# Four parts of the last v product among the first score blocks of a hybrid layer

## The chip, the core and the metric

The kernel runs on one core of a Trainium2 chip. The metric is the time of one execution on the device in microseconds (us). The core has five engines with instruction streams of their own: PE (TensorE, matrix products and transposes), DVE (VectorE), ACT (ScalarE), POOL (GpSimd) and SP (SyncE, which here only issues DMAs). They meet through semaphores alone.

## What is computed

One step of an encoder layer on 1024 prompt tokens and 32 sample tokens, model width 1024: a SwiGLU block, a mixer with three groups of heads, a second SwiGLU block and a norm. The mixer's second group, "fox", is attention with eight heads of 64 and a forget gate. Cut to that group:

```
h = rms(x); proj = h @ w_in                       # q, k, v, f_logit among its columns
q = head_rms(q, gq);  k = head_rms(k, gk)
F = cumsum(log_sigmoid(f_logit + b_f))            # past rows ahead of it
s = q @ k^T * 64**-0.5 + F_q - F_k                # causal
y = softmax(s) @ v
outputs also: k, v and log f of every token
```

## The kernel before

All 1056 tokens (1024 and 32) are handled together, with features on the partitions. The mixer runs over eight steps: two for the convolution, four "fox" pairs of two heads each (`g` = 0 to 3, called the first to the fourth pair here), and two memory pairs. A pair has two halves.

**Projections.** For each pair nine products are made, q, k and v, each in three chunks of 384, 384 and 288 tokens: n = 0 to 8. A product is 24 matmuls: eight blocks of the model width (`KT` = 8), and for each block three matmuls that multiply split numbers (high by high, low by high, high by low; lines 252 to 254). The last of them, n = 8, is the third chunk of v, 128x288, and goes to bank 2. After n = 7 PE transposes four tiles of k (`turn_tokens(0)`), after n = 8 the other five (`turn_tokens(1)`, `(2)`).

**Maxima by query.** `scores(n)`, n = 0 to 17, gives the scores of one tile of queries of one head; `smax(n)` on DVE adds -F and takes the row maximum (line 1692, tile scores_minusF, in an order of its own: the units 0 and 1 are the sample tokens, 2 to 9 the first head's eight tiles, with 128 to 1024 keys). Two areas of PSUM serve them in turn: `scores(n)` waits for `smax(n-2)`. `scores(0)` waits for the rounded k (`khi`, ACT line 1130, tile k_hi_twice) and `scores(1)` for ACT's copies of all k tiles by token (line 1147, tile k_by_token), whose banks it overwrites. `turn_tokens(3)` to `(5)` transpose v, eight tiles and the last of 32 tokens; `(4)` and `(5)` wait for the third chunk of v to be copied out (`vcopied`, ACT line 1196, tile vT). `turn_max` (lines 2074, 2075) turns maxima into rows, and ACT copies these.

**Weighted sum.** When the first head's maxima are all turned and copied, `keyed(0)` starts (line 2102). From there PE makes scores by key, ACT their exponentials, and PE the sums with v (line 2118); the second head's `scores(10)` to `(17)` stand among them. The next pair's nine products follow on PE.

The order on every engine is written out by hand; nothing is scheduled. On DVE the roundings of k (`k_twice`, `k_lo`, lines 1664 and 1671) stand right ahead of `smax(0)`. On ACT the stream in the loop over n is: copy v's chunk, round k after n = 7 (`k_hi`), copy tile groups (`tokens`). POOL rounds the next pair's weights when the ninth product and `k_lo` are done (lines 799 to 803). In the first pair only, PE also transposes the forget gates by token (line 2150); only after the first of these may SP load minusF (-F of a head, on every partition), which `smax(0)` waits for: it issues it at line 636.

Of the kernel before, what the change touches and what calls it, by code (L numbers as in the profile page):

```python
# [31 lines left out]
def hybrid_step(nc, i, o):  # L32
# [12 lines left out]
    KT = D // P  # L45
# [17 lines left out]
    with ctx:  # L63
# [78 lines left out]
        hh = sb("h_hi", [P, KT, T], F32R, ms_)  # L142
        hl = sb("h_lo", [P, KT, T], F32R, ms_)
# [112 lines left out]
        block = ctx.enter_context(nc.Block())  # L256
# [9 lines left out]
        def span(kind, n):  # L266

            what, _, c = PROJ[kind][n]
            return (0, NMEM) if kind == "mem" and what != "q" else CHUNKS[c]
# [583 lines left out]
        def _(act):  # L853
# [256 lines left out]
            def attend(g):  # L1110
                kind, it = ATTEND[g]
# [29 lines left out]
                def tokens(q):  # L1141
                    what, t0, nt, b = TT[kind][q]
                    act.wait_ge(A["tturned"], tt0 + q + 1)
                    n = tile_rows(kind, t0)
                    src = bank(b, nt * P, n).rearrange("p (t n) -> p t n", t=nt)
                    if what == "k":
                        act.activation(ktok[0:n, t0:t0 + nt, :], src, ACT.Copy).then_inc(A["tcopied"], 1)
                        return
                    for j in range(PAIR):
                        mm = act.activation(VO[0:n, t0:t0 + nt, j, half_rows(j)], src[:, :, half_rows(j)], ACT.Copy)  # L1150
                    mm.then_inc(A["tcopied"], 1)
# [40 lines left out]
                for n, (what, _, c) in enumerate(PROJ[kind]):  # L1192
                    s, w = span(kind, n)
                    act.wait_ge(A["proj"], proj0 + n + 1)
                    if what == "v":
                        act.activation(vT[:, s:s + w], bank(PBANK[kind][n], w), ACT.Copy).then_inc(A["vcopied"], 1)
                    else:
                        m = NORMED[kind].index(n)
                        if m >= 2:
                            act.wait_ge(A["sums"], sq0 + m - 1)  # L1200
                        act.activation(hsq[:, m % 2, 0:w], bank(PBANK[kind][n], w), ACT.Square)\
                            .then_inc(A["squares"], 1)
                    for m in SUMS_AFTER[kind].get(n, []):
                        head_rough(m)
                    if g == 0 and n == 1:
                        forget_log()
                    if n == (4 if kind == "fox" else 3):
                        past_keys()
                    if kind == "mem" and it == 0 and n == 1:
                        for h in range(2):  # L1210
                            act.wait_ge(mp["dve"], 5 + h)
                            act.activation(memh[:, 4 * h:4 * h + 4, :], memf[h], ACT.Copy).then_inc(mp["hi"], 1)
                    if n in (2, 3, 4):
                        q_hi(n - 2)
                    if kind == "fox" and n == 7:
                        k_hi()
                        act.wait_ge(A["stored"], upto(NSTORED, g))
                        tokens(0)
                    if kind == "fox" and n == 8:
                        tokens(1)  # L1220
                        tokens(2)
                if kind == "mem":
                    k_hi()
                    act.wait_ge(A["stored"], upto(NSTORED, g))
                    tokens(0)
                    tokens(1)
                else:
                    tokens(3)
                    tokens(4)
                    tokens(5)  # L1230
                for x in range(3):
# [552 lines left out]
        def _(pe):  # L1784
# [25 lines left out]
                pe.wait_ge(NORM[n]["sums"], sums_before(n, c) + 3)  # L1810
                pe.matmul(bank(MBANK + c, w), onesD[:, :], nsum[:, 0:w], start=True, stop=True).then_inc(NORM[n]["mean"], 1)

            def product(b, block, x_hi, x_lo, s, w, fresh=None):


                for k in range(KT):
                    if fresh:
                        n, c = fresh
                        pe.wait_ge(NORM[n]["lo"], KT * c + k + 1)
                    ks = slice(k * P, (k + 1) * P)  # L1820
                    mm = split3(pe, bank(b, w), whi[:, block, ks], wlo[:, block, ks], x_hi[:, k, s:s + w],
                                x_lo[:, k, s:s + w], k == 0, k == KT - 1)
                return mm
# [159 lines left out]
            def attend(g):  # L1983
# [137 lines left out]
                for n, (what, b, c) in enumerate(PROJ[kind]):  # L2121
                    s, w = span(kind, n)
                    pe.wait_ge(W["lo"], 3 * v + b + 1)
                    bank_free(n)
                    xh, xl = x.get((kind, what), (hh, hl))
                    if (kind, it) == ("mem", 0) and n == 3:
                        pe.wait_ge(mp["lo"], 2)
                    if (kind, it) == ("mem", 0) and n in (2, 3):
                        pe.wait_ge(mp["dve"], 6)
                    product(PBANK[kind][n], b, xh, xl, s, w).then_inc(A["proj"], 1)  # L2130
                    for m in SUMS_AFTER[kind].get(n, []):
                        head_sums(m)
                    if n == (4 if kind == "fox" else 3):
                        turn_past()
                    if (kind, it) == ("mem", 0) and n == 1:
                        pe.wait_ge(A["mixed"], 18 * g)
                        turn_memory()
                    if kind == "fox" and n == 7:
                        turn_tokens(0)
                if kind == "fox":  # L2140
                    turn_tokens(1)
                    turn_tokens(2)
                    if g == 0:
                        pe.wait_ge(fg["dve"], 10)
                        pe.wait_ge(A["tcopied"], 1)
                        for n, (src, at) in enumerate(((FL, 320), (FN, 400))):
                            for t in range(NT + n):
                                c0, w = (t * P, P) if t < PT else ((SEQ + PAST, DEC), (SEQ, PAST))[t - PT]
                                b = 512 * 3 + at + t * FH
                                mm = pe.transpose(PS[0:w, b:b + FH], src[:, c0:c0 + w], ident[0:FH, 0:FH])  # L2150
                            mm.then_inc(fg["turned"], 1)
                else:
                    turn_tokens(0)
                    turn_tokens(1)
                scores(0)
                scores(1)
                if kind == "fox":
                    turn_tokens(3)
                scores(2)
                scores(3)  # L2160
                if kind == "fox":
                    turn_tokens(4)
                scores(4)
                if kind == "fox":
                    turn_tokens(5)
                pe.wait_ge(A["vcopied"], upto(NV, g + 1))
                turn_max(0, 2, 0)
                turn_max(1, 2, DEC).then_inc(A["mturned"], 1)
# [84 lines left out]
```

## Time and profile before

| | |
|---|---|
| median of 3 runs | 2306.92 us (2306.61 to 2307.15) |
| the profiled execution | 2311.69 us |
| its span, first to last instruction | 2309.6 us |
| PE busy | 92% |
| DVE busy | 49% |
| ACT busy | 34% |
| mean granted TensorE clock | 0.946 |

The rows further below come from that one profiled execution. Its own time is 4.77 us above the median, and 2.1 us of it lie outside the span. A timeline row gives start, duration, engine, line, operation, output and inputs, shapes and count; in square brackets is the idle time ahead of it on its engine, and what ended it. The ends of matmuls are modelled and overlap; starts are the better measure of how they follow each other.

### The profile page before, as it was taken

How to read it: one execution, taken by the hardware profiler on the slowest of the kernel's cores; microseconds unless marked ns; L12 is line 12 of the kernel's file. 1: busy time of each engine (PE TensorE's matmuls, PEld its weight loads, DVE VectorE, ACT ScalarE, POOL GpSimd, SP SyncE). 2: the span in 40 equal slices, each digit the busy share in tenths (PEclk: the TensorE clock that was granted, in tenths of full speed). 3: DMA queues.
4: the chain of work that ended last, by engine and by line, in shares of the span. 5: the costliest groups of instructions: out<-in, count | busy, mean ns of one | idle time of the engine just before them, and what ended most of it. 6: DMA issues, size and time to landing. Idle time of an engine off the chain costs nothing.

```text
span 2309.6 us, 36830 instructions
## 1 busy us (share of the span) xinstructions
PE 2117.2 (92%) x15188; PEld 1995.8 (86%) x15188; DVE 1134.0 (49%) x1989; ACT 781.1 (34%) x1315; POOL 346.0 (15%) x175
## 2 busy tenths in 40 slices
PE   4599999999999888899999789966999999999996
PEld 4599999999999888776876567965999999999996
DVE  6855566556320162544544555177655665643103
ACT  5332222324221230454455453043232232433213
POOL 0000000004444522101101202000000000144440
PEclk7799999999999989899999779977999999999997
DMA  4512222228532326321220125032222222385222
GB/s 149 140 57 83 84 79 89 70 76 310 166 122 92 112 36 40 88 61 41 57 61 22 46 90 177 9 104 84 77 72 84 84 74 90 115 296 168 87 70 85
DMA packets 214774, 222.16 MB, mean 96 GB/s; under 512 B 27913, under 2 KB 156553, under 8 KB 214097
## 3 DMA queue, kind: packets, MB, share of 16 engines
q1 hardware_dynamic: 214608, 219.81, 31.5%
q8 instruction: 122, 2.00, 0.4%
q14 instruction: 44, 0.35, 0.0%
HBM read 169.98 MB, written 49.80 MB: 95 GB/s over the span
## 4 chain that ended last, share of the span: by engine, by line
PE 85%; DVE 7%; DMA 3%; ACT 2%; issue 1%; SPq 1%; POOL 0%; DVEq 0%; ACTq 0%
PE banks L252 24%; PE banks L253 24%; PE banks L254 24%; PE banks L2118 4%; PE banks L2060 1%; PE banks L2102 1%; PE banks L1831 1%; DMA x_again<-x_spill 1%; PE banks L2103 1%; DVE scores_minusF L1692 1%; DMA out_conv_state_sample<-conv_in 1%; PE banks L1997 1%; DVE hforms_lo L1459 1%; DVE hforms_f L1443 1%; PE banks L2218 0%
## 5 line engine op out<-in xcount | busy, mean ns | idle before, releaser
L252 PE MATMUL banks<-hforms_hi,w_hi 128*128 128x264 f32 x2112 | 604.8, 286 | 65.6 <-DVE hforms_lo L1459 44.6
L253 PE MATMUL banks<-hforms_lo,w_hi 128*128 128x264 f32 x2112 | 605.8, 287 | 0.0
L254 PE MATMUL banks<-hforms_hi,w_lo 128*128 128x264 f32 x2112 | 604.1, 286 | 0.0
L252 PEld LDWEIGHTS banks<-hforms_hi,w_hi 128*128 128x128 f32 x2112 | 402.5, 191 | 68.8 <-issue 35.7
L779 POOL TENSOR_TENSOR w_lo<-w_raw,w_hi 128x1024 fp32r<-128x1024 f32 x88 | 218.6, 2486 | 1386.6 <-ACT w_hi L984 1386.6
L254 PEld LDWEIGHTS banks<-hforms_hi,w_lo 128*128 128x128 f32 x2112 | 401.9, 190 | 0.0
L253 PEld LDWEIGHTS banks<-hforms_lo,w_hi 128*128 128x128 f32 x2112 | 401.5, 190 | 0.0
L254 PE MATMUL banks<-acts_a,w_lo 128*128 128x264 f32 x896 | 256.3, 286 | 0.0
L252 PE MATMUL banks<-acts_a,w_hi 128*128 128x264 f32 x896 | 254.2, 284 | 1.9 <-DVE acts_a L1477 1.9
L253 PE MATMUL banks<-acts_a,w_hi 128*128 128x264 f32 x896 | 255.0, 285 | 0.0
L252 PE MATMUL banks<-h_hi,w_hi 128*128 128x384 f32 (+1 forms) x576 | 198.8, 345 | 21.7 <-DVE h_lo L1311 10.0
L984 ACT ACTIVATE w_hi<-w_raw 128x1024 fp32r<-128x1024 f32 x88 | 93.2, 1059 | 349.8 <-PE banks L254 308.1
L253 PE MATMUL banks<-h_lo,w_hi 128*128 128x384 f32 (+1 forms) x576 | 189.6, 329 | 0.0
L254 PE MATMUL banks<-h_hi,w_lo 128*128 128x384 f32 (+1 forms) x576 | 188.7, 328 | 0.0
L252 PEld LDWEIGHTS banks<-acts_a,w_hi 128*128 128x128 f32 x896 | 170.0, 190 | 2.4 <-issue 2.4
L1493 DVE SCALAR_TENSOR_TENSOR xT<-banks,xT 128x264 f32<-128x264 f32 x64 | 23.9, 432 | 298.0 <-PE banks L254 298.0
L254 PEld LDWEIGHTS banks<-acts_a,w_lo 128*128 128x128 f32 x896 | 168.3, 188 | 0.0
L253 PEld LDWEIGHTS banks<-acts_a,w_hi 128*128 128x128 f32 x896 | 168.2, 188 | 0.0
L254 PE MATMUL banks<-acts_b,w_lo 128*128 128x264 f32 x512 | 146.5, 286 | 0.0
L253 PE MATMUL banks<-acts_b,w_hi 128*128 128x264 f32 x512 | 145.7, 285 | 0.0
L252 PE MATMUL banks<-acts_b,w_hi 128*128 128x264 f32 x512 | 145.1, 283 | 0.0
L252 PEld LDWEIGHTS banks<-h_hi,w_hi 128*128 128x128 f32 x576 | 111.5, 194 | 30.3 <-issue 20.8
(257 smaller groups left out, 3963.6 us busy)
## 6 DMA issues: line engine op xcount, KB each, us to landing
w_raw<-in_w_ffn_down SPq DMA_DIRECT2D x88, 512.0 KB, 4.2
w_raw<-in_w_ffn_gate SPq DMA_DIRECT2D x48, 512.0 KB, 5.2
w_raw<-in_w_ffn_up SPq DMA_DIRECT2D x48, 512.0 KB, 5.2
act_rows<-act_f SPq DMA_DIRECT2D x44, 528.0 KB, 2.8
acts_f<-act_rows SPq DMA_DIRECT2D x44, 528.0 KB, 5.0
xT<-x_spill SPq DMA_DIRECT2D x3, 4224.0 KB, 16.4
w_raw<-in_w_in SPq DMA_DIRECT2D x20, 512.0 KB, 5.9
x_spill<-xT SPq DMA_DIRECT2D x4, 2112.0 KB, 9.3
```

The lines of the kernel that those rows point to most:

```text
L252: eng.matmul(out, w_hi, x_hi, start=first, stop=False, skip_group_check=added)
L253: eng.matmul(out, w_hi, x_lo, start=False, stop=False, skip_group_check=added)
L254: return eng.matmul(out, w_lo, x_hi, start=False, stop=last, skip_group_check=added)
L779: pool.tensor_tensor(wlo[:, e % 4, :], raw[:, e % 4, :], whi[:, e % 4, :].bitcast(F32), ALU.subtract)\
L984: act.activation(whi[:, e % 4, :], raw[:, e % 4, :], ACT.Copy).then_inc(f["wd_hi"], 1)
L1443: dve.scalar_tensor_tensor(q[:, first:last + 1:last - first, :], x.rearrange("p (h n) -> p h n", h=2), gain[:, 2 * n, k:k + 1], nr[:, s:s ...
L1459: dve.tensor_tensor(HL[z][:, :, kk, :], FT[:, m % 2, 0:7, :], HH[z][:, :, kk, :].bitcast(F32), ALU.subtract).then_inc(f["forms_lo"], 1)
L1493: dve.scalar_tensor_tensor(xT[:, d, s:s + QC], bank(DBANK[e], QC), 0.5, xT[:, d, s:s + QC], ALU.mult, ALU.add).then_inc(f["resid"], 1)
L1692: dve.tensor_tensor_reduce(junk[0:rows, 0:w], PS[0:rows, b:b + w], nF[0:rows, j, k0:k0 + w], 1.0, -3e38, ALU.add, ALU.max, m).then_inc(A[" ...
L1831: mm = pe.matmul(bank(4 + c, QC), onesD[:, :], q[:, k, :], start=k == 0, stop=k == KT - 1)
L1997: pe.matmul(bank(6 + m % 2, w), onesH[:, :], hsq[:, m % 2, 0:w], start=True, stop=True)\
L2118: pe.matmul(PS[:, 512 * ob + oc:512 * ob + oc + w], VO[0:kr, vo, j, :], PRT[0:kr, (b0 + n) % 4, 0:w], start=first, stop=last, skip_group_c ...
```

## The change

The ninth product of a fox pair is no longer made whole behind the eighth. The loop over n ends at n = 8, `product` takes the blocks that it shall do, and `last_v` makes two of the eight blocks (six matmuls) at a time: one part ahead of `scores(0)`, one behind `turn_tokens(3)`, one behind `scores(2)`, one behind `scores(3)`. The product's semaphore follows the fourth part. `turn_tokens(1)` and `(2)` now stand ahead of all parts, and so do, in the first pair, the transposes of the forget gates. `turn_tokens(4)` and `(5)` stand together behind `scores(4)`. ACT copies k's tiles and the first four of v ahead of v's third chunk. The memory pairs keep their order. Lines below the edit have other numbers: PE's line 2035 is 2032 afterwards, 2060 is 2057, 2063 is 2060, 2150 is 2154.

```diff
@@ ACT, attend(g) @@
                     if kind == "fox" and n == 7:
                         k_hi()
                         act.wait_ge(A["stored"], upto(NSTORED, g))
-                        tokens(0)
-                    if kind == "fox" and n == 8:
-                        tokens(1)
-                        tokens(2)
+                        for q in range(4):
+                            tokens(q)
...
                 else:
-                    tokens(3)
                     tokens(4)
                     tokens(5)
@@ PE @@
-            def product(b, block, x_hi, x_lo, s, w, fresh=None):
+            def product(b, block, x_hi, x_lo, s, w, fresh=None, steps=range(KT)):
...
-                for k in range(KT):
+                for k in steps:
...
+                    if kind == "fox" and n == 8:
+                        break
                     product(PBANK[kind][n], b, xh, xl, s, w).then_inc(A["proj"], 1)
...
+                def last_v(steps):
+
+                    s, w = span(kind, 8)
+                    return product(PBANK[kind][8], 2, hh, hl, s, w, None, steps)
...
                             mm.then_inc(fg["turned"], 1)
+                    last_v(range(0, 2))
+                    scores(0)
+                    scores(1)
+                    turn_tokens(3)
+                    last_v(range(2, 4))
+                    scores(2)
+                    last_v(range(4, 6))
+                    scores(3)
+                    last_v(range(6, KT)).then_inc(A["proj"], 1)
+                    scores(4)
+                    turn_tokens(4)
+                    turn_tokens(5)
                 else:
                     turn_tokens(0)
                     turn_tokens(1)
-                scores(0)
-                scores(1)
-                if kind == "fox":
-                    turn_tokens(3)
-                scores(2)
-                scores(3)
-                if kind == "fox":
-                    turn_tokens(4)
-                scores(4)
-                if kind == "fox":
-                    turn_tokens(5)
+                    for n in range(5):
+                        scores(n)
```

PE in the third pair before, from the ninth product's last matmul to `scores(4)` (the rows with k_hi_twice and mask_bf are the score blocks, those with ident and vT the transposes of v; an "x4" means four in a row):

```order
L254 MATMUL banks<-h_hi,w_lo 128x288
L2035 MATMUL banks<-ident,kT 128x128 x4
L2035 MATMUL banks<-ident,kT 32x128
L2060 MATMUL banks<-k_hi_twice,q_hi_lo 32x160
L2063 MATMUL banks<-mask_bf,ident_bf 32x32
L2060 MATMUL banks<-k_hi_twice,q_hi_lo 32x160
L2063 MATMUL banks<-mask_bf,ident_bf 32x32
L2035 MATMUL banks<-ident,vT 128x128 x4
L2060 MATMUL banks<-k_hi_twice,q_hi_lo 128x128
L2063 MATMUL banks<-mask_bf,ident_bf 128x128
L2060 MATMUL banks<-k_hi_twice,q_hi_lo 128x256
L2063 MATMUL banks<-mask_bf,ident_bf 128x128
```

The same engine and pair now, from `turn_tokens(3)` to the score block of 128x128 (`scores(2)`):

```order
L2032 MATMUL banks<-ident,vT 128x128 x4
L252 MATMUL banks<-h_hi,w_hi 128x288
L253 MATMUL banks<-h_lo,w_hi 128x288
L254 MATMUL banks<-h_hi,w_lo 128x288
L252 MATMUL banks<-h_hi,w_hi 128x288
L253 MATMUL banks<-h_lo,w_hi 128x288
L254 MATMUL banks<-h_hi,w_lo 128x288
L2057 MATMUL banks<-k_hi_twice,q_hi_lo 128x128
L2060 MATMUL banks<-mask_bf,ident_bf 128x128
```

Six matmuls of the product stand ahead of `scores(2)`, where none stood; six more stand ahead of `scores(3)`, and six ahead of `scores(4)`.

ACT in the third pair before, from the rounding of k to the copies of v by token:

```order
L1130 ACTIVATE k_hi_twice<-kT 64x1184 x2
L1147 ACTIVATE k_by_token<-banks 128x512
L1196 ACTIVATE vT<-banks 128x288
L1147 ACTIVATE k_by_token<-banks 128x512
L1147 ACTIVATE k_by_token<-banks 32x128
L1150 ACTIVATE v_and_ones<-banks 128x4x64 x4
L1150 ACTIVATE v_and_ones<-banks 32x64 x2
```

And now:

```order
L1130 ACTIVATE k_hi_twice<-kT 64x1184 x2
L1147 ACTIVATE k_by_token<-banks 128x512 x2
L1147 ACTIVATE k_by_token<-banks 32x128
L1150 ACTIVATE v_and_ones<-banks 128x4x64 x2
L1196 ACTIVATE vT<-banks 128x288
L1150 ACTIVATE v_and_ones<-banks 128x4x64 x2
L1150 ACTIVATE v_and_ones<-banks 32x64 x2
```

The copy of v's third chunk (vT, 128x288) has moved behind all copies of k and the first two of v.

PE in the first pair before, behind the ninth product, with the forget gates (logf_rows, minusF_rows):

```order
L254 MATMUL banks<-h_hi,w_lo 128x288
L2035 MATMUL banks<-ident,kT 128x128 x4
L2035 MATMUL banks<-ident,kT 32x128
L2150 MATMUL banks<-ident,logf_rows 128x8 x8
L2150 MATMUL banks<-ident,logf_rows 32x8
```

And now, behind the eighth product:

```order
L254 MATMUL banks<-h_hi,w_lo 128x384
L2032 MATMUL banks<-ident,kT 128x128 x8
L2032 MATMUL banks<-ident,kT 32x128
L2154 MATMUL banks<-ident,logf_rows 128x8 x8
L2154 MATMUL banks<-ident,logf_rows 32x8
```

The forget gates' transposes are ahead of the whole ninth product now.

## Rows read from the trace of the kernel before

**Rows 1.** The page: the chain that ended last, by engine.
```profile
PE 85%; DVE 7%; DMA 3%; ACT 2%; issue 1%; SPq 1%; POOL 0%; DVEq 0%; ACTq 0%
```

**Rows 2.** Timeline of the third pair, all engines, up to the first maximum.
```profile
1133.79 0.60 PE L2035 MATMUL banks<-ident,kT 128*128 128x128 f32 x4
...
1134.37 2.40 ACT L1130 ACTIVATE k_hi_twice<-kT 64x1184 fp32r<-64x1184 f32 x2
1135.59 2.81 DVE L1671 TENSOR_TENSOR k_lo_and_one<-kT,k_hi_twice 64x1184 fp32r<-64x1184 f32 x2 [0.98 <-ACT k_hi_twice L1130]
1136.79 0.60 ACT L1147 ACTIVATE k_by_token<-banks 128x512 f32<-128x512 f32 x1
...
1137.40 0.71 PE L2035 MATMUL banks<-ident,kT 128*128 128x128 f32 x5
1137.60 0.41 ACT L1196 ACTIVATE vT<-banks 128x288 f32<-128x288 f32 x1 [0.21 <-PE banks L254]
...
1137.87 0.32 PE L2060 MATMUL banks<-k_hi_twice,q_hi_lo 128*32 128x160 f32 x1
1138.04 0.74 ACT L1147 ACTIVATE k_by_token<-banks 128x512 f32<-128x512 f32 x2
...
1138.43 0.31 DVE L1692 CUSTOM_DVE_ANT_0 scores_minusF<-banks,minusF 32x160 f32<-32x160 f32 x1
```

**Rows 3.** The chain that ended last, in order of time, in the ninth product.
```profile
1137.17 0.13 PE banks L252
...
1137.43 0.13 PE banks L254
```

**Rows 4.** Timeline of the third pair, from `scores(1)` to the maximum of unit 5.
```profile
1138.83 0.26 PE L2060 MATMUL banks<-k_hi_twice,q_hi_lo 128*32 128x160 f32 x1 [0.54 <-ACT k_by_token L1147]
...
1139.97 0.29 DVE L1692 CUSTOM_DVE_ANT_0 scores_minusF<-banks,minusF 128x128 f32<-128x128 f32 x1 [0.40 <-PE banks L2063]
...
1140.38 0.42 PE L2060 MATMUL banks<-k_hi_twice,q_hi_lo 128*128 128x384 f32 x1
...
1141.11 0.49 PE L2060 MATMUL banks<-k_hi_twice,q_hi_lo 128*128 128x512 f32 x1
...
1141.71 0.69 DVE L1692 CUSTOM_DVE_ANT_0 scores_minusF<-banks,minusF 128x512 f32<-128x512 f32 x1 [0.15 <-PE banks L2063]
```

**Rows 5.** Timeline of the third pair, from the last maximum of the first head.
```profile
1145.88 1.22 DVE L1692 CUSTOM_DVE_ANT_0 scores_minusF<-banks,minusF 128x1024 f32<-128x1024 f32 x1
...
1147.17 0.32 PE L2074 MATMUL banks<-ident,row_max 128*65 128x128 f32 x1 [1.05 <-DVE row_max L1692]
...
1148.17 0.50 PE L2102 MATMUL banks<-q_hi_lo,k_hi_twice 128*128 128x512 f32 x1 [0.68 <-ACT q_hi_and_max L1164]
```

**Rows 6.** PE by stretches: length, busy (instructions), granted clock, DMA share, GB/s.
```profile
1138.00:1139.00 1.00, 0.46 (x4) 1.00 0.00 0
1145.80:1148.10 2.30, 0.64 (x2) 1.00 0.00 0
1149.00:1153.00 4.00, 4.00 (x14) 0.57 0.00 0
961.00:972.00 11.00, 8.19 (x31) 0.53 1.10 294
```

**Rows 7.** Timeline of the first pair: ACT, SP's queue, DVE and PE.
```profile
955.41 0.60 ACT L1147 ACTIVATE k_by_token<-banks 128x512 f32<-128x512 f32 x1
...
956.65 0.68 PE L2150 MATMUL banks<-ident,logf_rows 8*128 8x8 f32 x9
...
957.41 0.81 SPq L636 DMA_DIRECT2D minusF<-negF_rows  x2
...
963.42 0.31 DVE L1692 CUSTOM_DVE_ANT_0 scores_minusF<-banks,minusF 32x160 f32<-32x160 f32 x1 [4.90 <-DMA minusF<-negF_rows]
...
963.79 0.47 PE L2060 MATMUL banks<-k_hi_twice,q_hi_lo 128*128 128x128 f32 x1 [4.67 <-DVE row_max L1692]
...
967.68 0.69 DVE L1692 CUSTOM_DVE_ANT_0 scores_minusF<-banks,minusF 128x512 f32<-128x512 f32 x1 [0.80 <-PE banks L2063]
```

## The prediction

> **What bounds the kernel now.** I read the page's chain first: PE carries 85% of it and DVE 7% [rows 1], so what is not PE's own rate is mostly waits for DVE. A pair's timeline shows where DVE is the bound: between the end of the nine products and `keyed(0)`. In the third pair the ninth product's last matmul starts at 1137.43 and is done at 1137.56 [rows 3], and `keyed(0)` starts at 1148.17 [rows 5]; in 10.6 us PE has only score blocks and transposes to make. The first, second and fourth pairs have the same stretch, in the second and fourth with the same waits to 0.02 us.
>
> The reader should see who holds that stretch. ACT's rounding of k ends at 1134.37 + 2.40 = 1136.77, DVE's `k_lo` ends at 1135.59 + 2.81 = 1138.40, and the first maximum starts at 1138.43, 0.03 us later [rows 2]. So at its start the chain of maxima is bound by DVE's `k_lo`, not by the ninth product, which ran beside it: **the product is hidden today**. The end is 1145.88 + 1.22, then a transpose at 1147.17 and ACT's copy [rows 5]. In between DVE is nearly gapless: it waits 0.50 us for the second unit (`scores(1)` could start only at 1138.83, after ACT's copies of k [rows 4]), 0.40 us for the third and 0.15 us for the sixth [rows 4]. That is 1.05 us in all, which is all that a perfect feed by PE could save in a pair.
>
> **What the change does in the second to fourth pair.** The step is 24 matmuls, spaced 0.13 us (1137.17 to 1137.43 is two of them [rows 3]): 3.1 us of PE. None is removed. I go along PE with the third pair's times.
>
> *Ahead of `scores(0)`.* The four transposes at 1133.79 are over by 1134.37; the five others take 0.45 us more (1137.40 to 1137.87 [rows 2]), so the first part runs from 1134.85 to 1135.65. Then `scores(0)` waits for the rounded k until 1136.8. PE idles 1.2 us where it had the product. The first maximum stays at 1138.43, since `k_lo` is untouched: gain nothing, loss nothing.
>
> *`scores(1)`.* It waits for three copies of k tiles. ACT had v's chunk (0.41 us) and a wait for it between them; now they go 1136.79 + 0.60 + 0.74 = 1138.13 [rows 2]. So `scores(1)` starts at 1138.19, 0.64 us earlier than 1138.83 [rows 4], and DVE's first gap of 0.50 us closes. Between `scores(0)` and this PE idles another 1.0 us.
>
> *`scores(1)` to `scores(5)`.* Before: 1141.11 - 1138.83 = 2.28 us [rows 4]. Added: 18 matmuls by 0.131 = 2.36 us, some 0.1 us for three switches (an estimate: 0.03 us a switch, from the starts around the product), and the copy of v's third chunk. That copy now follows the product's end directly and `turn_tokens(4)` waits for it: 0.41 us and some 0.2 us of latency [rows 2], less the 0.33 us of `scores(4)` between them, so 0.3 us. That is 5.04 us, and `scores(5)` starts at 1138.19 + 5.04 = 1143.23, 2.12 us later than 1141.11. The sixth maximum moves from 1141.71 to 1143.83 with it.
>
> *Behind it.* From the sixth maximum on DVE goes without gaps (five of them, 5.4 us to 1147.10), each unit's scores being ready two ahead. Nothing is given back, so `keyed(0)` is **2.1 us later** in each of three pairs: 6.4 us. ACT's v copies and the stores through SP's queue move too, but `keyed(0)` has them done by 1146. POOL starts the next pair's weights some 3.5 us later, and they take 10.3 us; the next products come some 35 us after that, which covers it. Queued behind PE's waits in this piece are only score blocks, and DVE waits for those alone.
>
> Bounds for one pair: 2.36 - 0.64 = 1.7 us, if switches and the copy cost nothing, and 2.5 us, if the copy's wait is twice as long. I take 2.1.
>
> **The first pair** is bound by a DMA. The first maximum waits 4.90 us for minusF, whose load SP issues at 957.41, when the first transposes of the forget gates are done [rows 7]. These now need only ACT's first copy (955.41 + 0.60 = 956.01) and no longer stand behind five transposes, so they start at 956.05 instead of 956.65: 0.6 us earlier, and minusF and the first maximum too (962.8). The first two parts lie in waits. The other two come behind the DMA's end, at a time when PE's clock has fallen: from 961 to 972 it was granted 0.53 of full speed [rows 6], that is, 1.2 GHz after 4.67 us without work [rows 7]. Now PE would be idle for some 3.1 us there. At half clock 12 matmuls are 12 by 0.26 = 3.1 us, with the copy's wait 3.4 us, less 0.6: +2.8 us at the sixth maximum. At full clock the whole would be faster than now, since from the first to the sixth maximum the third pair takes 3.28 us and this one 4.26 [rows 2, 4, 7]: 3.28 + 1.6 + 0.3 less the 0.9 us of the early transposes and of ACT's copies is 4.3, so -0.6, and 0.7 us more from larger units at full clock: -1.3. The row it is nearest to is the fallen clock, and part of the late maxima may then already run at 2.4 GHz: I take **+2.3 us**, with -1.3 and +2.8 as ends.
>
> **The clock in the new gaps.** Today PE idles 1.05 and 0.68 us ahead of `keyed(0)` [rows 5] and is busy 0.64 of 2.30 us there; the clock then falls to 1.2 GHz, and over 4.00 us it is 0.57 [rows 6]: 4.0 by 0.43 = 1.7 us of full work lost. All four pairs show it. The short gap at 1138 (busy 0.46 of 1.00 us) drew no fall [rows 6]. The new gaps, 1.2 and 1.0 us around `scores(0)`, are as deep as the first kind. A fall right behind them meets the stretch where PE is the bound, so it costs the same 1.7 us. It depends on how the gaps lie; I expect it in two of three pairs, and that one of the present falls behind the maxima fails to come, as places shift: **net one, +1.7 us**, between -1.7 and +5.1.
>
> The Trainium skill (TensorE: Matmul & The Clock Gate, "What's actually happening") says that the activity monitor runs free and does not start anew with the kernel, so that the number of slow matmuls differs between runs. By that rule this term is a draw of each run rather than a fixed cost; the runs of before, within 0.54 us of each other, do not show such a spread.
>
> **The sum.** 6.4 + 2.3 + 1.7 = +10.4 us. Against the profiled execution that is a span of 2309.6 + 10.4 = 2320.0; the difference goes over to the median, 2306.92 + 10.4 = **2317.3 us**.
>
> **The rivals.**
> *A, no new fall of the clock.* The new gaps leave the clock up and the first pair's shorter idle too: 6.4 - 1.3 = +5.1, 2312.0 us. For it: a shorter gap at 1138 drew none. Against it: gaps of this depth did, four times.
> *B, not slower.* The parts keep PE busier just ahead of `keyed(0)`, and the falls of the clock behind the maxima no longer come. Each is worth 1.7 us [rows 6], so from A all four give 5.1 - 6.8 = -1.7, 2305.2 us; it decides from the third one on. For it: those falls are a matter of how little PE does. Against it: the 2.1 us that are idle or nearly so behind the last score block are the same, and the parts end 4 us earlier.
> *C, two falls in a row.* The half clock lasts over all of `scores(1)` to `scores(5)`, 3.9 us of work in three pairs: 6.4 + 2.8 + 11.7 = +20.9, 2327.8 us. For it: in the first pair PE was busy at half clock for eight of the eleven us and did not recover [rows 6]. Against it: 1149 to 1153 is one short fall.
> The Trainium skill (Perfetto Trace Analysis, "Matmul Optimizations") says that the engine scales with its use and that matmuls should run back to back in batches, which speaks against cutting this product; by that rule the outcome would be C's.
> *D, the parts fill gaps after all.* DVE's 1.05 us of gaps are closed and the parts cost PE nothing. That would need the score blocks two units ahead of DVE at units 2 to 4; with 0.29 to 0.56 us a unit on DVE and 0.8 us a part on PE they cannot be. It would give 2306.92 - 3.2 = 2303.7 us.
>
> **How the numbers follow.** Main case 0.62 (2313 to 2321), A 0.17, B 0.08, C 0.08, D 0.02, rest 0.03. A measurement of this kernel can tell 0.2%, 4.6 us, from no change: slower means over 2311.5. The main case, C and most of A are slower: 0.80. Within 0.2%: the low side of A and most of B, 0.15. Faster: D and some of B, 0.05. The range runs from 2309 to 2322; it leaves out C, D and most of B.
>
> **What the profile of after would show.** For the steps: a third pair in which the first maximum still follows `k_lo` by 0.03 us, the second one without a gap, gaps of DVE of about 1.0, 0.6 and 0.7 us ahead of the third to fifth and some 0.9 ahead of the sixth, `turn_tokens(4)` waiting for vT, and 2.1 us more from `k_lo` to `keyed(0)`; SP's minusF 0.6 us earlier in the first pair; a clock of 0.5 somewhere between `scores(1)` and `scores(5)`. It would be wrong if the first maximum itself moved (ACT's or DVE's part would then not be what holds it), or if the maxima behind the sixth had gaps that took up the delay.

## The result, and the profile after

The changed kernel takes 2320.66 us (median of 5 runs, 2314.54 to 2323.07) against 2307.15 us before (5 runs, 2306.61 to 2309.01). The ratio is 1.005, 95% interval 1.0037 to 1.0063: slower by half a percent. The profiled execution is at 2323.07 us, the slowest of the five; its span is 2321.0 us against 2309.6. These five runs lie 8.5 us apart, the five of before 2.4. That alone does not make the spread a mark of the change: in three later sets of runs the kernel before was itself 6.6, 12.2 and 5.5 us apart (35, 29 and 15 runs).

The page of after; busy times of PE, DVE and ACT are as before to 2 us, so no engine does more. The second row is the chain by engine, to be held against [rows 1]:

```profile
span 2321.0 us, 36830 instructions
...
PE 86%; DVE 6%; ACT 3%; DMA 2%; issue 2%; POOL 0%; SPq 0%; DVEq 0%; ACTq 0%
```

Time is best read from two distances that every fox pair has: from the start of `k_lo` on DVE to the start of `keyed(0)` on PE (the stretch that the change touches), and from there to the next pair's `k_lo` (the weighted sum and eight products, which it does not touch). Worked out from the timelines, in us:

| pair | k_lo to keyed(0), before | after | keyed(0) to next k_lo, before | after |
|---|---|---|---|---|
| first | 20.68 | 22.39 | 73.32 | 74.30 |
| second | 12.59 | 16.29 | 74.80 | 73.30 |
| third | 12.58 | 14.72 | 73.38 | 73.33 |
| fourth | 12.59 | 16.25 | | |

The first two columns differ by 1.71 + 3.70 + 2.14 + 3.66 = 11.21 us, the last two by -0.57. Ahead of the first `k_lo` after is 1.46 us late (955.66 against 954.20), behind the fourth `keyed(0)` 0.72 us short. Together that is the span's 11.38 us. So the loss is where the change is.

The third pair of after, which answers to [rows 2] and [rows 4], with DVE, PE and ACT; `k_lo` is line 1668 here and the maxima 1689, score blocks are line 2057:

```profile
1141.94 2.80 DVE L1668 TENSOR_TENSOR k_lo_and_one<-kT,k_hi_twice 64x1184 fp32r<-64x1184 f32 x2 [0.98 <-ACT k_hi_twice L1130]
...
1143.37 0.23 PE L2057 MATMUL banks<-k_hi_twice,q_hi_lo 128*32 128x160 f32 x1 [1.30 <-DVE k_lo_and_one L1668]
...
1144.42 0.26 PE L2057 MATMUL banks<-k_hi_twice,q_hi_lo 128*32 128x160 f32 x1 [0.70 <-ACT k_by_token L1147]
...
1144.77 0.31 DVE L1689 CUSTOM_DVE_ANT_0 scores_minusF<-banks,minusF 32x160 f32<-32x160 f32 x1
...
1146.35 0.29 DVE L1689 CUSTOM_DVE_ANT_0 scores_minusF<-banks,minusF 128x128 f32<-128x128 f32 x1 [0.79 <-PE banks L2060]
...
1147.38 0.42 DVE L1689 CUSTOM_DVE_ANT_0 scores_minusF<-banks,minusF 128x256 f32<-128x256 f32 x1 [0.74 <-PE banks L2060]
...
1148.23 0.41 ACT L1196 ACTIVATE vT<-banks 128x288 f32<-128x288 f32 x1 [2.15 <-PE banks L254]
...
1148.48 0.56 DVE L1689 CUSTOM_DVE_ANT_0 scores_minusF<-banks,minusF 128x384 f32<-128x384 f32 x1 [0.66 <-PE banks L2060]
1148.69 0.77 PE L2032 MATMUL banks<-ident,vT 128*128 128x128 f32 x5 [0.25 <-ACT vT L1196]
...
1150.19 0.69 DVE L1689 CUSTOM_DVE_ANT_0 scores_minusF<-banks,minusF 128x512 f32<-128x512 f32 x1 [1.15 <-PE banks L2060]
```

PE stands still for 1.30 us where the product was, and for 0.70 us behind `scores(0)`. (The profile names `k_lo` as what released `scores(0)`; by the times it is ACT's rounding of k, which ends at the same moment.) DVE starts its maxima 2.83 us after `k_lo`'s start, as before, and then waits for PE four times: 0.79, 0.74, 0.66 and 1.15 us, where it waited 0.40, 0, 0 and 0.15.

In the second and fourth pair the clock fell in addition. (A "fall" here is a stretch in which the granted clock of PE is at 1.2 instead of 2.4 GHz, that is, 0.5 in the profile.) PE by stretches (length, busy, granted clock, DMA share, GB/s), four us from about `scores(1)` on in the second, third and fourth pair:

```profile
1055.00:1059.00 4.00, 4.00 (x21) 0.57 0.46 135
1145.00:1149.00 4.00, 3.75 (x31) 1.00 0.50 139
1232.50:1236.50 4.00, 4.00 (x20) 0.57 0.46 135
```

At 0.57 PE gets through 21 and 20 instructions, at full clock through 31. These two pairs take 16.29 and 16.25 us and the third 14.72: a fall costs 1.55 us there.

### The profile page after: what moved, and what is told of

Read it like the earlier page. It is cut to its first block, busy times and chain, and to the rows that moved or that the text cites. A ratio compares the mean times of both kernels' runs of the same rounds, so it can differ in the third digit from the quotient of the medians.

```text
span 2321.0 us, 36830 instructions
## 1 busy us (share of the span) xinstructions
PE 2119.2 (91%) x15188; PEld 1997.7 (86%) x15188; DVE 1134.0 (49%) x1989; ACT 780.5 (34%) x1315; POOL 345.8 (15%) x175
## 4 chain that ended last, share of the span: by engine, by line
PE 86%; DVE 6%; ACT 3%; DMA 2%; issue 2%; POOL 0%; SPq 0%; DVEq 0%; ACTq 0%
PE banks L252 25%; PE banks L253 25%; PE banks L254 25%; PE banks L2115 4%; PE banks L1828 1%; PE banks L2099 1%; PE banks L2057 1%; DVE scores_minusF L1689 1%; DMA x_again<-x_spill 1%; PE banks L2100 1%; DMA out_conv_state_sample<-conv_in 1%; PE banks L1994 1%; DVE hforms_lo L1456 1%; DVE hforms_f L1440 1%; PE banks L1793 0%
```

## The experiments

The medians of the kernel before were not the same in all sets of runs (2308.47, 2311.69 and 2311.14 us in the three below; 2307.15 above), so each run is judged by its ratio to the runs of before of its own set, and by the two distances in its profile. Several expectations gave absolute times from the 2307 us of before and miss for that reason alone; where a miss means more, it is said.

**The theory.** The ninth product is free where it was, since DVE's `k_lo` ends later than it; behind the first score block it is paid in full, since DVE then works on units shorter than a part. The clock's fall in the new gap comes on top. **Rivals**: ACT's new order is what delays; the cut as such or the wait for v's copy, not the amount of late matmuls; the clock alone.

**The whole product ahead of `scores(0)`.** The rest of the change stays.

```diff
-                    last_v(range(0, 2))
+                    last_v(range(0, KT)).then_inc(A["proj"], 1)
                     scores(0)
                     scores(1)
                     turn_tokens(3)
-                    last_v(range(2, 4))
                     scores(2)
-                    last_v(range(4, 6))
                     scores(3)
-                    last_v(range(6, KT)).then_inc(A["proj"], 1)
                     scores(4)
```

> The changed kernel with one edit: the ninth product stands whole ahead of scores(0), as before; the transposes of k (and in the first pair those of the forget gates) ahead of it and ACT's new order stay. Theory (the product is free ahead of k_lo's end and dear behind it): the three late parts gone, so from k_lo to keyed(0) some 0.5 us less than the kernel before in the second to fourth pair (scores(1) no longer waits for ACT), no clock fall ahead of the maxima; 2304.5 to 2307 us. Rival (the transposes' and ACT's new places cost the time): near the changed kernel, 2314 us or more. Rival (clock falls alone cost it): like the first.

Measured: 2308.76 us (11 runs) against 2308.47, ratio 1.0002 (0.9993 to 1.0011). The whole loss is gone. (The expected 2304.5 to 2307 us was missed.) From `k_lo` to `keyed(0)` it is 12.62, 12.61 and 12.61 us in the second to fourth pair. The second to fifth maximum follow without a gap, the sixth has one:

```profile
1137.30 0.31 DVE L1689 CUSTOM_DVE_ANT_0 scores_minusF<-banks,minusF 32x160 f32<-32x160 f32 x1
...
1140.61 0.69 DVE L1689 CUSTOM_DVE_ANT_0 scores_minusF<-banks,minusF 128x512 f32<-128x512 f32 x1 [0.79 <-PE banks L2060]
```

So it is the product's move behind `scores(0)` that costs, by its late parts and by the gap that it leaves, and not the new places of k's transposes or ACT's new order, which both stay in this kernel. The next experiments part the two terms. The expected gain of 0.5 us a pair did not come: what the second and third unit saved, the sixth lost. That gap is taken up below.

**One late part instead of three.**

```diff
-                    last_v(range(0, 2))
+                    last_v(range(0, 6))
                     scores(0)
                     scores(1)
                     turn_tokens(3)
-                    last_v(range(2, 4))
                     scores(2)
-                    last_v(range(4, 6))
                     scores(3)
                     last_v(range(6, KT)).then_inc(A["proj"], 1)
```

> The changed kernel with six blocks (18 matmuls) ahead of scores(0) and only the last two (6 matmuls) behind scores(3). Theory: a dose of one part of three. The part itself costs 0.8 us and the copy of v's chunk 0.3, less the 0.5 to 0.6 of the earlier scores(1) and what DVE's gap at the third unit takes up: +0.3 to +0.7 us in each of the second to fourth pair, no fall of the clock in front; 2307 to 2310 us. Rival (it is the copy's wait and the cut, not the amount of late matmuls): close to the changed kernel's +2.1 a pair, 2313 us or more.

Measured: 2311.62 us (12 runs), ratio 1.0013 (1.0002 to 1.0024). The distances are 13.45, 13.59 and 13.44 us, +0.9 over before and +0.8 over the whole product ahead, for six late matmuls. That is a little over what was expected, since the sixth maximum's gap is in it. Late matmuls and delay: 0 give +0.03 us a pair, 6 give +0.9, 18 give +2.1. The delay follows the amount, about 0.8 us for the first six (0.79 us of PE) and 1.25 us for twelve more (1.6 us of PE). The rival that blames the cut falls: with one late part the wait for v's copy and a switch are there, and the delay is 0.9 us and not 2.1.

**The gap filled.** Two extra pieces of six matmuls in each fox pair, ahead of the first part.

```diff
+                    last_v((0, KT - 1))
+                    last_v((0, KT - 1))
                     last_v(range(0, 2))
                     scores(0)
```

> The changed kernel with 12 more matmuls of 128x288 (into bank 2, overwritten later) at the place where PE waits for the rounded k. They are extra work in a gap of 1.3 us and end 0.3 us after it, with 1.4 us left to k_lo's end. Theory (two terms: the late parts, +2.1 a pair, and falls of the clock in the new gap, +1.6 each, in one to three pairs of a run): no half clock between scores(1) and scores(5), the +2.1 stays; 2313 to 2316 us and less spread than the 2314.5 to 2323.1 of the changed kernel. Rival (clock alone): back to 2307. Rival (late parts alone): as the changed kernel or later by the filler.

Measured: 2313.58 us (11 runs), ratio 1.0022 (1.0013 to 1.003), against 1.005 of the changed kernel. The second to fourth pair are all at 14.72 us, and none has a fall between `k_lo` and `keyed(0)`. About the same stretch as above, in this kernel:

```profile
1049.00:1053.00 4.00, 3.50 (x28) 1.00 0.48 135
1137.00:1141.00 4.00, 3.44 (x27) 1.00 0.46 135
1225.00:1229.00 4.00, 3.43 (x28) 1.00 0.50 139
```

Twelve matmuls of pure extra work in each pair make the kernel faster than the changed one. That parts the two terms for the second to fourth pair: 2.13 us belong to the late parts, 1.55 us to a fall. Of the 10.2 us between the spans of the two profiles (2321.0 and 2310.8), the two falls are 3.1. Another 5.0 come from the first pair (19.82 and 71.86 us instead of 22.39 and 74.30), where the wait for a load differs too, so not all of the rest is the clock. Less spread, which was expected, was not seen: 2309.33 to 2318.49 us.

**The product cut short.** The kernel before, with two of the ninth product's eight blocks; six blocks of v's third chunk are left out.

```diff
-            def product(b, block, x_hi, x_lo, s, w, fresh=None):
...
-                for k in range(KT):
+            def product(b, block, x_hi, x_lo, s, w, fresh=None, steps=range(KT)):
...
+                for k in steps:
...
-                    product(PBANK[kind][n], b, xh, xl, s, w).then_inc(A["proj"], 1)
+                    product(PBANK[kind][n], b, xh, xl, s, w, None,
+                            (0, KT - 1) if kind == "fox" and n == 8 else range(KT)).then_inc(A["proj"], 1)
```

> The kernel before with the ninth product of a fox pair cut to two of its eight blocks (6 matmuls instead of 24; this part of the computation is left out). Theory (the product is hidden under the rounding of k): 18 matmuls, 2.36 us a pair and 9.4 us in all, less work on PE, yet keyed(0) no more than 0.6 us earlier after k_lo; total -2 us at most, and a fall of the clock in the new gap may even take that back: 2304 to 2311 us. Rival (PE's rate bounds the stretch): 2297.5 us.

Measured: 2310.93 us (11 runs) against 2308.47, ratio 1.0006 (0.9998 to 1.0015): 9.4 us of PE's work gone, and nothing gained. In the fourth pair, with no fall ahead of `keyed(0)`, the distance is 12.13 us instead of 12.59: of the 2.36 us taken away at most 0.46 were not hidden. They are the part of DVE's waits for the second and third unit that ACT's earlier copies of k close (0.50 and 0.40 us before, none and 0.29 here). The second and third pair are even slower for the product's absence, 13.62 and 13.64 us, since the clock falls behind the gap that it leaves. All three pairs have that gap, 1.3 and 1.0 us, so it does not draw a fall each time. Two stretches, third and fourth pair:

```profile
1137.00:1142.00 5.00, 4.49 (x23) 0.66 0.37 108
1225.00:1229.00 4.00, 3.75 (x29) 1.00 0.72 187
```

**The changed kernel once more.**

> The changed kernel once more, beside the others of this job. Theory (late parts, +2.1 in each of the second to fourth pair, plus falls of the clock in the new gap that come in one to three pairs of a run): 2314 to 2323 us, and in its profile each pair's time from k_lo to keyed(0) either 14.7 us (no fall) or about 16.3 us (fall). Rival (the spread has another cause): values of a pair between these two or outside.

Measured: 2323.29 us (5 runs, 2318.45 to 2327.31) against 2311.69, ratio 1.0049 (1.0037 to 1.0061). The profile is of the slowest run, above the expected 2314 to 2323. Its pairs are at 16.29, 14.71 and 16.26 us: the two values expected and no other, and in the same pairs as in the first profile. Whether the number of falls is what spreads the runs is not shown: both profiles, 4 us apart, have the same two falls ahead of `keyed(0)`, and beside them the kernel before, which has no such gap, lay between 2306.27 and 2318.47 us.

**ACT's order alone.** PE as before.

```diff
                     if kind == "fox" and n == 7:
                         k_hi()
                         act.wait_ge(A["stored"], upto(NSTORED, g))
-                        tokens(0)
-                    if kind == "fox" and n == 8:
-                        tokens(1)
-                        tokens(2)
+                        for q in range(4):
+                            tokens(q)
...
-                    tokens(3)
                     tokens(4)
                     tokens(5)
```

> The kernel before with only the change's order on ACT: all copies of k and the first of v ahead of the copy of v's third chunk. PE as before. Theory: turn_tokens(4) stands ahead of scores(4) and waits for that copy, which now follows the first v copies: 1139.84 + 0.66 + 0.41 = 1140.9 instead of an issue at 1140.0, so some +0.5 to +0.9 us a pair in the second to fourth, and +1.5 to +3 us in all: 2309.5 to 2311.5. Rival (ACT's order is what delays the changed kernel): +2 us a pair, 2315. Rival (free): 2308.

Measured: 2314.63 us (12 runs) against 2311.69, ratio 1.0013 (1.0004 to 1.0021). The pairs take 13.49, 13.47 and 13.47 us, +0.9 each, which is the top of what was expected: the copy of v's third chunk now waits for `turn_tokens(3)` and the copies behind it, and `turn_tokens(4)` ahead of `scores(4)` waits for the copy:

```profile
1140.39 0.56 DVE L1689 CUSTOM_DVE_ANT_0 scores_minusF<-banks,minusF 128x384 f32<-128x384 f32 x1 [0.95 <-PE banks L2060]
```

ACT's order is dear with PE's old order. In the changed kernel it is cheap: there ACT waits 2.15 us for the product before the copy, and PE then waits 0.25 us for it (the rows of the third pair above). So it is not the changed kernel's +2.1.

The profile shows one thing more. It is of the fastest of the twelve runs (2307.33 us), and in all four of its pairs the clock stays up behind `keyed(0)`: 71.87, 71.86 and 71.85 us to the next `k_lo`, with the waits of 1.05 and 0.68 us ahead of `keyed(0)` as before in the second to fourth pair and no extra work in them. So these waits do not draw a fall each time either; what decides it stays open.

**The v copy ahead of the v tiles**, on top of the whole product ahead.

```diff
                     if kind == "fox" and n == 7:
                         k_hi()
                         act.wait_ge(A["stored"], upto(NSTORED, g))
-                        for q in range(4):
+                        for q in range(3):
                             tokens(q)
...
+                    tokens(3)
                     tokens(4)
                     tokens(5)
```

> The kernel with the ninth product whole ahead of scores(0) (measured at 12.61 us from k_lo to keyed(0), gap of 0.80 us ahead of the sixth maximum), but ACT copies v's third chunk ahead of the v tiles. Theory (that gap is the five transposes standing together behind scores(4), not ACT's copy): the gap stays at 0.6 to 0.8 us, 12.4 to 12.6 us. Rival (the copy of v's chunk is what PE waits for): gap under 0.3 us, 12.0 us.

Measured: 2309.96 us (11 runs) against 2311.14, ratio 0.9998 (0.999 to 1.0007); 12.38 us in each pair. The gap ahead of the sixth maximum goes from 0.79 to 0.57 us:

```profile
1138.92 0.69 DVE L1690 CUSTOM_DVE_ANT_0 scores_minusF<-banks,minusF 128x512 f32<-128x512 f32 x1 [0.57 <-PE banks L2061]
```

A good quarter of that gap is ACT's copy; the rest is put down to the five transposes that stand together ahead of `scores(5)`, and the next run moves them. (The expectation's lower bound of 0.6 was just missed.)

**An order by DVE's slack.** From the kernel with the whole product ahead, with ACT as in the last one:

```diff
                     scores(4)
-                    turn_tokens(4)
-                    turn_tokens(5)
+                    scores(5)
+                    turn_tokens(4)
+                    scores(6)
+                    turn_tokens(5)
...
                 turn_max(1, 2, DEC).then_inc(A["mturned"], 1)
-                for n in range(5, 8):
-                    scores(n)
-                turn_four(0, 0)
-                scores(8)
+                if kind == "fox":
+                    scores(7)
+                    scores(8)
+                    turn_four(0, 0)
...
                 scores(9)
                 turn_four(0, 1)
```

> An order from the reasons found: the ninth product whole ahead of scores(0); transposes of k ahead of it; turn_tokens(4) behind scores(5), turn_tokens(5) and turn_max behind scores(6), turn_four(0,0) behind scores(8), where DVE's units take 0.8 us and more and leave PE room; ACT copies v's third chunk ahead of all v tiles. Theory (PE has to be two units ahead of DVE only while units are short): no gap of DVE over 0.3 us between the ten maxima in the second to fourth pair, sixth maximum 5.5 to 5.7 us behind k_lo's start instead of 6.1, keyed(0) 0.5 to 0.7 us earlier a pair; with the first pair -2 to -3.5 us: 2305 to 2306.5. Rival (the maxima's end is held by ACT's copies or the turn of the maxima): no gain, 2308.

Measured: 2308.01 us (11 runs) against 2311.69, ratio 0.9983 (0.9975 to 0.9992). All of the second to fourth pair are at 11.96 us, 0.63 less than before, and DVE has no gap left between its ten maxima:

```profile
1136.79 0.31 DVE L1690 CUSTOM_DVE_ANT_0 scores_minusF<-banks,minusF 32x160 f32<-32x160 f32 x1
1137.26 0.31 DVE L1690 CUSTOM_DVE_ANT_0 scores_minusF<-banks,minusF 32x160 f32<-32x160 f32 x1
1137.72 0.29 DVE L1690 CUSTOM_DVE_ANT_0 scores_minusF<-banks,minusF 128x128 f32<-128x128 f32 x1
1138.16 0.42 DVE L1690 CUSTOM_DVE_ANT_0 scores_minusF<-banks,minusF 128x256 f32<-128x256 f32 x1
1138.74 0.56 DVE L1690 CUSTOM_DVE_ANT_0 scores_minusF<-banks,minusF 128x384 f32<-128x384 f32 x1
1139.45 0.69 DVE L1690 CUSTOM_DVE_ANT_0 scores_minusF<-banks,minusF 128x512 f32<-128x512 f32 x1
```

The ratio is a little more than the expected gain; the absolute time lies above the expectation, which had the 2307 us of before in it.

**PE filled ahead of `keyed(0)`.** The kernel before, with seven extra matmuls of 128x512 in each fox pair.

```diff
                     for t in range(4):
+                        if kind == "fox" and (j, h, t) == (0, 1, 3):
+                            filler(4)
                         mm = turn_max(2 + PT * j + 4 * h + t, (2, 3, 7, 7)[2 * j + h], t * P)
                     mm.then_inc(A["mturned"], 1)
+                    if kind == "fox" and (j, h) == (0, 1):
+                        filler(3)
+
+                def filler(n):
+                    for _ in range(n):
+                        pe.matmul(bank(0, 512), Q1[:, 0, 0:P], KS1[:, 0, 0:512], start=True, stop=True)
```

> The kernel before with seven more matmuls of 128x512 into a free bank in each fox pair, four ahead of the last transpose of the maxima and three behind it, where PE idles 1.05 and 0.68 us: extra work, overwritten later. Theory (idle PE of that depth makes the clock fall, and each fall costs up to 1.7 us of work in the weighted sum behind it): no half clock in the 7 us behind keyed(0) in any fox pair, 4 falls gone: -3 to -7 us, 2301 to 2305. Rival (falls come with the weighted sum's own waits, or cost nothing since ACT bounds it): 2307.5 to 2309.

Measured: 2305.99 us (11 runs) against 2311.69, ratio 0.9975 (0.9967 to 0.9984). The falls behind `keyed(0)` are gone in all four pairs; the time is 5.7 us less, within the 3 to 7 expected. Eight us of the weighted sum, this kernel (second and third pair), and the kernel before (second and fourth):

```profile
1063.00:1071.00 8.00, 7.85 (x37) 1.00 0.01 2
1147.00:1155.00 8.00, 7.85 (x38) 1.00 0.00 0
```

```profile
1060.00:1068.00 8.00, 7.32 (x22) 0.57 0.01 2
1235.00:1243.00 8.00, 7.85 (x33) 0.81 0.00 0
```

From `keyed(0)` to the next `k_lo` it is 71.87, 71.86 and 71.86 us, where before had 73.32 with a short fall and 74.80 with one of twice the length (0.57 over these eight us instead of 0.81). A short fall costs 1.46 us here, less than the 1.7 us of work that it delays.

One profile without falls would prove little, since that of ACT's order alone has none either. Taken over all profiles it does: in the ten without this extra work the granted clock of the eight us behind `keyed(0)` is 0.58 to 0.79 in 34 of 40 pairs and 1.00 in six; in the two with it (this one and the next) it is 1.00 in eight of eight. The medians agree.

**Both in one.** The last two edits together.

> Both of the last two edits in one kernel: the order by DVE's slack (ninth product whole ahead of scores(0), transposes of v later, k_lo to keyed(0) 11.96 us in its profile) and the seven extra matmuls ahead of keyed(0) (keyed(0) to the next k_lo 71.86 us without a fall of the clock). Theory (the terms add): 11.96 and 71.86 us in each pair, 0.63 us and 1.46 us less than the kernel before a pair that had one fall; some -7 us in all, ratio 0.997. Rival (the terms overlap, since an earlier keyed(0) only waits longer for something else): no better than 0.9975.

Measured: 2302.75 us (5 runs, 2298.85 to 2304.43) against 2311.14, ratio 0.9963 (0.9949 to 0.9976). The distances are 11.96 us three times and 71.87, 71.89 and 71.87 us: they add. This is faster than both kernels of the study.

## Why the prediction was right

It gave 2317.3 us (2309 to 2322) and slower; the median is 2320.66, near the upper end. Run once more it was 2323.29, above the range, beside a kernel before that was 4.5 us slower as well; the ratio was the same. Step by step:

- **What bounds the stretch.** Right: in the second to fourth pair the first maximum stays 2.83 to 2.85 us behind `k_lo`'s start in all kernels, and the kernel with the product cut short shows that the product was hidden but for at most 0.46 us. One row was misread, and nothing rests on it: the product's last matmul starts at 1137.27, and the 1137.43 of the chain is the start of its last 0.13 us.
- **The second to fourth pair, +2.1 us each.** Right to the digit where the clock stays up: 14.72 - 12.58 = 2.14 us in the third pair, 2.13 in all three with the gap filled. The gaps of DVE were forecast as 1.0, 0.6, 0.7 and 0.9 us and came as 0.79, 0.74, 0.66 and 1.15. The sum is right because it was made along PE. One thing in it went unseen: five transposes together ahead of `scores(5)` cost DVE 0.57 us by themselves, also with the product out of the way. They were counted in PE's time and not named as a cost of the change.
- **Nothing given back.** Right: from the sixth to the last maximum 4.18 us after, 4.17 before.
- **The first pair, +2.3 us.** Measured +1.71 in the stretch, by another way, so that the size is near is in part luck. SP did issue the load of minusF earlier against `k_lo` (by 2.68 us behind it instead of 3.21), as forecast, but the first maximum came 7.12 us behind the issue instead of 6.01, so it was 0.58 us later and not 0.6 earlier. The wait for minusF, which this pair hangs on:

```profile
958.34 0.81 SPq L636 DMA_DIRECT2D minusF<-negF_rows  x2
...
965.46 0.31 DVE L1689 CUSTOM_DVE_ANT_0 scores_minusF<-banks,minusF 32x160 f32<-32x160 f32 x1 [6.01 <-DMA minusF<-negF_rows]
```

  In the ten other profiles of changed kernels the first maximum is between 8.70 and 10.59 us behind `k_lo`. The step took the load's time as fixed, and it varies by more than what was argued about. From there to `keyed(0)` it is 12.59 us against 11.46: +1.1 instead of +2.9. The clock was down only for a part of it, 0.81 of full speed on average from 965.50 to 978.00 us, where the kernel before had 0.63 from 963.40 to 974.90.
- **The clock in the new gaps, net +1.7 us.** The count was right, two of three pairs, and the price nearly (1.55 us instead of 1.7): +3.1. Behind the maxima no fall failed to come, but that of the second pair was half as long (74.80 to 73.30 us), which comes to the same, and the first pair got a dearer one (73.32 to 74.30). Net +2.5. The mechanism is right, the number in part luck: waits of one and the same size drew a fall in some pairs and not in others, and nothing in the trace said in which.
- **The sum.** Forecast 6.4 + 2.3 + 1.7 = 10.4, measured 6.4 + 1.7 + 2.5 and 0.7 from places that the change does not touch: 11.4 us of span, unrounded. The median is 13.5 us above that of before (11.6 when it was run once more). The forecast took a difference read from an execution at 2311.69 us over to a median of 2306.92; which falls the faster runs of before had is not known, so what the 13.5 is made of beyond the 11.4 stays open.
- **The rivals.** A would need pairs without falls: only the third was one. B (the falls behind `keyed(0)` vanish as PE is fed more) did not happen, though the kernel filled ahead of `keyed(0)` shows that its mechanism exists when the feed comes in the right place. C, two falls in a row ahead of `keyed(0)`, did not show. The Trainium skill's page "TensorE: Matmul & The Clock Gate", section "What's actually happening", says that the activity monitor runs free of the kernel's start. What the runs here show of it is mixed: that equal waits drew a fall behind `keyed(0)` in 34 of 40 pairs, and in none of the four of one profile, would fit a draw of each run, while both profiles of the changed kernel had their falls ahead of `keyed(0)` in the same pairs. The prediction held the 0.54 us between three runs of before against such a draw; 29 later runs of it lay 12.2 us apart. D is ruled out by DVE's four gaps.

## What to carry to other kernels

Work that PE did beside a longer step of another engine was all but free here, and moving it into a chain where PE feeds that engine in short units made it dear: before splitting a product to "fill gaps", ask which gap it leaves and whose turn it is where it goes. Put side work of the feeder behind the long units of the consumer, not between the short ones; here that closed all of DVE's gaps. Judge a fall of the clock by several profiles, since one may have none by chance. And a gap that looks harmless on the path may be paid later by the clock, so that even useless matmuls in it can be worth their time.

## What was not expected of the hardware

Taking 18 of the 24 matmuls of a hidden product away in each pair, 9.4 us of PE's time, did not make the kernel faster (1.0006): no more than 0.46 us a pair was to be had, and behind the gap of 1.3 and 1.0 us the granted clock fell in two of three pairs, which cost more. And 28 extra matmuls of 128x512 made it 0.25% faster (0.9975, 0.9967 to 0.9984): with PE kept busy through 1.05 and 0.68 us of waits, the clock stayed at 2.4 GHz behind them in all four pairs, where it had fallen to 1.2 GHz in all four in the profile of before. Without extra work there, waits of this size (0.83 to 1.05 and 0.68 us) drew a fall in 34 of 40 pairs over ten profiles.
